# Attention over all keys: which engine copies the turned groups of a C map out of PSUM

## The reference

```python
def gqa_attend(q, k, v):                                   # group A
    s = jnp.einsum('bqhgd,bshd->bhgqs', q, k) * (q.shape[-1] ** -0.5)
    p = jax.nn.softmax(s, axis=-1)
    return jnp.einsum('bhgqs,bshd->bqhgd', p, v)

def diff_attend(q, k, v, lam):                             # group C
    s1 = jnp.einsum('bqhd,bshd->bhqs', q[..., 0, :], k[..., 0, :]) * scale
    s2 = jnp.einsum('bqhd,bshd->bhqs', q[..., 1, :], k[..., 1, :]) * scale
    a = jax.nn.softmax(s1, axis=-1) - lam * jax.nn.softmax(s2, axis=-1)
    return jnp.einsum('bhqs,bshd->bqhd', a, v)
...
    oc = rms_norm(oc, g_sub_c) * (1.0 - lam_init)
    y = jnp.concatenate([oa.reshape(b, t, A_WIDTH), ob, oc.reshape(b, t, C_WIDTH)], axis=-1)
    return y @ w_out
```

## Time and profile before

| | |
|---|---|
| runs, median (lowest to highest) | 3418.88 us (3418.83 to 3421.21, 3 runs) |
| the profiled execution: its own time | 3416.16 us |
| its span, from first to last instruction | 3414.3 us |
| mean granted TensorE clock, share of full speed | 0.975 |
| TensorE busy | 3188.8 us (93%) |
| VectorE busy | 2154.0 us (63%) |
| ScalarE busy | 1324.7 us (39%) |
| attention phase, layer 0, all 1280 keys | about 418 to 790 us |
| attention phase, layer 1 | about 2186 to 2560 us |

### The profile page before, as it was taken

How to read it: one execution, slowest core, us unless ns; L and a number is a source line. 1 busy time by engine, 2 the same in 40 slices (tenths; PEclk the granted TensorE clock), 3 DMA queues, 4 the chain that set the end, 5 groups by cost and what they waited for, 6 DMA issues and landing times. The chain is left out here.

```text
span 3414.3 us, 49517 instructions
## 1 busy us (share of the span) xinstructions
PE 3188.8 (93%) x18000; PEld 2566.9 (75%) x18000; DVE 2154.0 (63%) x3314; ACT 1324.7 (39%) x2061; POOL 1126.8 (33%) x1155
## 2 busy tenths in 40 slices
PE   6989899999999999999998899899999699999996
PEld 4876577777788888888886686677777578888885
DVE  4654587886644444444446764578875667777777
ACT  3431476764422211111112441476664333333332
POOL 1333355552110000000002332355551465555653
PEclk9989999999999999999999999999999899999998
DMA  6557401104221111111105466201013111111113
GB/s 240 194 189 272 141 21 35 35 20 170 105 62 37 37 37 37 37 37 37 40 27 189 151 219 244 110 33 35 32 57 143 65 53 55 52 46 54 53 52 117
DMA packets 189958, 304.92 MB, mean 89 GB/s; under 512 B 13447, under 2 KB 139919, under 8 KB 178535
## 3 DMA queue, kind: packets, MB, share of 16 engines
q1 hardware_dynamic: 187685, 302.04, 25.7%
q10 hardware_dynamic: 2113, 0.77, 0.1%
HBM read 234.58 MB, written 68.19 MB: 89 GB/s over the span
## 5 line engine op out<-in xcount | busy, mean ns | idle before, releaser
L132 PE MATMUL banks<-h_hT,up_u_hi 128*128 128x512 f32 (+1 forms) x1056 | 375.3, 355 | 7.2 <-DVE up_u_lo L2009 5.7
L133 PE MATMUL banks<-h_hT,up_u_lo 128*128 128x512 f32 (+1 forms) x1056 | 374.8, 355 | 0.0
L134 PE MATMUL banks<-h_hT,up_u_hi 128*128 128x512 f32 (+1 forms) x1056 | 374.6, 355 | 0.0
L132 PE MATMUL banks<-ff_d_lo,ff_a_hi 128*128 128x512 f32 x792 | 316.3, 399 | 25.4 <-DVE h_acc L3175 12.4
L134 PE MATMUL banks<-ff_d_hi,ff_a_hi 128*128 128x512 f32 x792 | 309.1, 390 | 0.0
L133 PE MATMUL banks<-ff_d_hi,ff_a_lo 128*128 128x512 f32 x792 | 309.0, 390 | 0.0
L2440 POOL TENSOR_TENSOR ff_ms<-ff_ss,c_eps 128x1 f32<-128x1 f32 x10 | 10.1, 1010 | 898.5 <-ACT ff_t_gate L2551 898.5
L2591 DVE TENSOR_TENSOR ff_acc<-banks,ff_acc 128x512 f32<-128x512 f32 x220 | 150.8, 689 | 175.2 <-PE banks L134 175.0
L1564 PE MATMUL banks<-c_ident,al_prA 128*128 128x128 f32 x1312 | 215.2, 278 | 20.1 <-ACT al_oTC L1867 18.7
L3175 DVE TENSOR_TENSOR h_acc<-banks,h_acc 128x512 f32<-128x512 f32 x336 | 225.0, 689 | 4.1 <-PE banks L134 0.9
L132 PEld LDWEIGHTS banks<-h_hT,up_u_hi 128*128 128x128 f32 x1056 | 200.3, 190 | 36.2 <-issue 5.9
(11 more groups left out here) (351 smaller groups left out, 8134.2 us busy)
## 6 DMA issues: line engine op xcount, KB each, us to landing
kv_m_wm<-in_w_mod_dram SPq DMA_DIRECT2D x40, 1024.0 KB, 4.9
up_u_raw<-in_w_up_dram SPq DMA_DIRECT2D x44, 512.0 KB, 3.9
ff_d_raw<-in_w_down_dram SPq DMA_DIRECT2D x44, 512.0 KB, 3.3
hT_d<-fr_hs SPq DMA_DIRECT2D x20, 1024.0 KB, 5.3
st_hs<-hT_d SPq DMA_DIRECT2D x20, 1024.0 KB, 7.0
q_d<-fr_qs SPq DMA_DIRECT2D x18, 512.0 KB, 3.1
q_d<-fr_qs SPq DMA_DIRECT2D x36, 256.0 KB, 2.9
al_quA<-q_d SPq DMA_DIRECT2D x18, 512.0 KB, 3.9
```

The costliest lines, as they stand in the source:

```text
L132: e.matmul(out, w[0], x[1], start=start, stop=False)
L133: e.matmul(out, w[1], x[0], start=False, stop=False)
L134: return e.matmul(out, w[0], x[0], start=False, stop=stop)
```

## The change

ScalarE copies C groups 1 and 0, in that order, behind `exp_a(n)`; VectorE copies group 2 alone. The order in which TensorE turns the groups and takes the banks stays as it was. The waits in `emptied` and ahead of the value products follow from the tables.

```diff
-    A_ACT, A_DVE, C_ACT, C_DVE = (0, 1), (2,), (0,), (1, 2)
+    A_ACT, A_DVE, C_ACT, C_DVE = (0, 1), (2,), (1, 0), (2,)
@@ vector, in the loop over n
-                if k is not None and 1 in groups_c(k):
-                    pc_out(k, 1)
                 if unit_at(n, O_A) is not None:
                     finish_a(unit_at(n, O_A))
@@ scalar
-            def pc_out(k):
+            def pc_out(k, g):
                 u = k // 2
                 if k % 2 == 0 and u >= 2:
                     e.wait_ge(pvC_done, u - 1)
-                ka, kb = groups_c(k)[0]
-                e.wait_ge(tC_done, turnsC[k, 0])
-                e.copy(ptC[:, ka:kb, u % 2, k % 2, :], bank("TC", k, 0)[:, 0:kb - ka, :]).then_inc(outC_act, 1)
+                ka, kb = groups_c(k)[g]
+                e.wait_ge(tC_done, turnsC[k, g])
+                e.copy(ptC[:, ka:kb, u % 2, k % 2, :], bank("TC", k, g)[:, 0:kb - ka, :]).then_inc(outC_act, 1)
@@ scalar, in the loop over n
                 if key_c(n) is not None:
-                    pc_out(key_c(n))
+                    for g in C_ACT:
+                        if g in groups_c(key_c(n)):
+                            pc_out(key_c(n), g)
```

## The result

| | before | changed |
|---|---|---|
| median (lowest to highest), 4 runs each | 3418.86 us (3416.18 to 3421.21) | 3477.65 us (3475.74 to 3481.18) |
| profiled execution: own time / span | 3416.16 / 3414.3 us | 3478.89 / 3477.0 us |
| mean granted TensorE clock | 0.975 | 0.976 |

The ratio on record is 1.0176, 95% interval 1.0162 to 1.0190 (the quotient of the two medians, 1.0172, lies inside it): the changed kernel is 58.8 us slower by the medians, 62.7 by the profiled executions. The forecast was 3479, range 3465 to 3497.

A forecast was written before the change was run, and what follows sets the result against it. TensorE was taken to bound the kernel. Late C group 2 starts add 76.2 us, less 14.4 absorbed by existing waits, so 61.8 us on 3416.16 gives 3478.0; the median was put at 3479 us, range 3465 to 3497.

The forecast's parts named there:

- What bounds the kernel: Attention over all keys: TensorE, busy 89.56 of 93 us in 16 steps, sets the step time of 5.81 us.
- VectorE's part costs nothing: VectorE loses 35.7 us of C group 1 copies; max_c can start at most 0.06 us earlier, counted at nothing.
- The wait ahead of C group 2: Even steps: TensorE starts C group 2 when C group 1's bank is handed back, about 0.15 us after the copy.
- The price of 1.27 us and the 60 places: C group 2 starts a mean 1.27 us later, behind ScalarE's exponential, in 60 even steps: 76.2 us.
- the 76.2 of the sum: Added TensorE delay over both layers before absorption: 60 even steps times 1.27 us.
- The absorbed part: TensorE's existing waits around steps like 31 and 33 swallow 10.8 + 3.6 = 14.4 us of the delay.
- the stall: TensorE's added wait ahead of C group 2, 1 to 1.27 us in each of 60 even steps; chance 0.90.
- The clock rival: New gaps lower TensorE's clock in attention steps, to a mean of 0.88: 3525 us (to 3570); chance 0.06.
- The faster hand takes the bank: ScalarE's shorter copy of C group 1 frees the bank earlier than now: 3407 to 3411 us; chance 0.02.

The follow-up runs named there:

- the run with groups 0 and 2: On the changed kernel, ScalarE copies C groups 0 and 2 and VectorE copies group 1, where it did before: 3416.39 us, ratio 0.9997.
- the better one: Kernel before with oT_c ahead of the C map's exponential, and C-output squares and normalizing behind max_a: 3378.10 us; with the change added, 3455.26 us.
- the run with the squares behind: On the kernel before, VectorE's squares and normalizing of the C output moved behind max_a: 3406.48 us, ratio 0.9970.

## Why the prediction was right, point by point

- *What bounds the kernel.* Right: TensorE's work stayed at 3189 us, and in the steps over all keys only the moves that brought the bank back late cost time. VectorE's and ScalarE's busy shares, 61% and 39% after, would have said that there is room on both.
- *VectorE's part costs nothing.* Right, shown from two sides: VectorE waits 0.48 us for `rest_c` in the copy's place, and with the copy gone but the bank on time (the copy ahead of the exponential) the time is that of before.
- *The wait ahead of C group 2.* Right in what it was used for: with the bank handed back in time there was no slack behind it, and each later hand-over cost its full length. The order of the two copies turned round moved the time by 25.5 us for the same work. But "there is one" was too strong for the kernel before: with the bank back 0.09 us sooner, C group 2 started only 0.01 us sooner. The bank and TensorE's own work were ready together. The forecast's price didn't suffer, because it took the difference of two starts and not the wait.
- *The price of 1.27 us and the 60 places.* Both measured: 1.27 us in step 34, and 60 waits that print about 1.1 us, 0.15 less than TensorE was late. Undiluted the change costs 76 to 77 us against the 76.2 of the sum.
- *The absorbed part.* Right in the sum, 14.4 us forecast and 76 to 77 less 59 to 63, so 13 to 18, measured. Three of its steps were off. The first is a cause: I put `max_a`'s lateness down to VectorE's queue, with the squares ahead of it; the squares themselves are stretched by GpSimd. It made no difference to the changed kernel, since TensorE comes later than either, and it made the expectation of the run with groups 0 and 2 miss by 8 us. The second: of the wait for `oTC` ahead of step 32 I took 0.1 us as absorbed, where it grew: 0.42 before, 0.58 after,

```profile
511.37 0.52 PE L1564 MATMUL banks<-c_ident,al_prA 128*128 128x128 f32 x3 [0.58 <-ACT al_oTC L1865]
```

as the step is now held by TensorE's own chain like step 28. The third: a step like 33 gave back more than the 0.28 us that the view printed. By the starts of steps, step 31 became 0.65 us shorter (6.51 to 5.86), step 33 0.38 shorter (8.31 to 7.93), and step 32 1.41 longer (4.67 to 6.08), 0.14 more than the stall. Over eight steps the forecast was 4 x 1.27 - 0.72 - 0.28 = 4.08 us, and 4.13 were measured. That the two agree so well is in part luck: what step 32 cost above the forecast, the other steps gave back for the larger part.
- *The clock rival.* Did not happen: the granted clock was 1.00 in the 101 us shown above, as in the 93 us before, and 0.976 over the program. What the Trainium skill tells ("TensorE: Matmul & The Clock Gate", section "A second HAM failure mode: psum-queue depth-cycling") of another kernel in bf16, that short idle times while it cycles through PSUM's banks make the clock go back and forth, isn't borne out by waits of 1.1 us in every second step of this one.
- *The faster hand takes the bank.* Did not happen, though its premise holds: ScalarE's copy is the shorter one (0.465 against 0.558 us). Where it comes at once, ahead of the exponential, step 34 is 0.03 us shorter (4.03 us against 4.06) and step 33 0.06 longer, and eight steps take 46.28 us against 46.27: nothing is gained.

## What to carry to other kernels

With a ring of buffers, the question about a copy here wasn't how long it takes or how busy its engine is, but what stands ahead of it in its queue when the buffer's next user arrives. Read the start of that user against the end of the copy, since a hand-over that is only just in time isn't printed as a wait. If work is to go to the less loaded engine, put the copy that somebody waits for ahead of the long instruction, and one for which there is time behind it. A stall first falls into the waits that the bound engine already has: the same edit cost 59 to 63 us on the kernel before and 76 to 77 on the better one. And where one wait stands behind another, both must be taken away before their full worth shows, 38.6 us here against 13.8 and 10.2.

## What the runs showed of the hardware

The two VectorE operations looked at here that have two inputs in SBUF didn't finish before the operation on SBUF that GpSimd had already begun. The squares (128x256) took 0.42 us free, and 1.00 and 1.60 us when begun 0.71 and 1.32 us ahead of GpSimd's end, each time ending 0.28 or 0.29 us behind it. The normalizing took 0.42 us free in the run with the squares behind, against 1.63 in the kernel before and 2.26 in the run with groups 0 and 2. `max_a`, which reads PSUM, kept its 1.47 us beside the same operation. The Trainium skill has this rule ("SBUF — State Buffer", section "Who interferes with whom": VectorE and GpSimd share a pair of ports as an exclusive lock, and a VectorE instruction with two SBUF inputs contends with a GpSimd instruction that reads SBUF). The rows agree: the squares and the normalizing, with two such inputs, are held, and `max_a`, with none, is not.
